# First attention by pairs of heads, and its output linear's first two tiles in parts

## The reference

```python
def diff_attention(h, w_qkv, w_o, lam_params, subln_g, rel_bias, lambda_init):
    qkv = h @ w_qkv
    ...
    logits = jnp.einsum('bqhmd,bkhmd->bhmqk', qb, k).astype(jnp.float32) * scale + bias
    logits = jnp.where(rel >= 0, logits, -jnp.inf)
    p = jax.nn.softmax(logits, axis=-1)
    w = p[:, :, 0] - lam * p[:, :, 1]
    return jnp.einsum('bhqk,bkhe->bqhe', w.astype(v.dtype), v)
    ...
    o = rms_norm(o, subln_g) * (1 - lambda_init)
    return o.reshape(b, s, A_V_WIDTH) @ w_o
```

## Time and profile before

| | |
|---|---|
| median of 3 runs | 2152.95 us (2150.6 to 2153.96) |
| profiled execution | 2148.51 us |
| its span, first to last instruction | 2146.7 us |
| PE busy | 1883.2 us (88%) |
| DVE busy | 1645.4 us (77%) |
| ACT busy | 876.8 us (41%) |
| POOL busy | 526.4 us (25%) |
| mean granted clock of PE | 0.938 |

### The profile page before, as it was taken

The page is one execution under the profiler, slowest core; times in us unless marked ns, Lnnn a source line. Parts: engine busy times, 40 slices in busy tenths (PEclk is TensorE's granted clock), DMA queues, the critical chain, the costliest instruction groups (busy, mean ns, idle before and its releaser), DMA issues.

```text
span 2146.7 us, 32722 instructions
## 1 busy us (share of the span) xinstructions
PE 1883.2 (88%) x12438; PEld 1589.1 (74%) x12438; DVE 1645.4 (77%) x2910; ACT 876.8 (41%) x1409; POOL 526.4 (25%) x464
## 2 busy tenths in 40 slices
PE   5999898999999998899999999999776766766676
PEld 5999897999999997899999999989422222222222
DVE  5887767887888877654569998758988877877765
ACT  3444465544555436654444445555212112212111
POOL 0111002111001110211120002332554455445451
PEclk7999999999999998999999999999988888888888
DMA  7889732678868884254544454536999999999996
GB/s 316 319 314 369 290 137 101 240 307 293 294 253 309 308 326 180 99 194 162 169 175 164 177 177 177 190 105 267 412 422 422 422 422 422 422 423 422 423 423 250
DMA packets 88787, 606.34 MB, mean 282 GB/s; under 512 B 9763, under 2 KB 11059, under 8 KB 21468
## 3 DMA queue, kind: packets, MB, share of 16 engines
q1 hardware_dynamic: 37708, 245.03, 31.8%
q0 software_dynamic: 37040, 270.57, 30.3%
q10 hardware_dynamic: 13920, 89.15, 10.3%
HBM read 601.53 MB, written 3.18 MB: 282 GB/s over the span
## 4 chain that ended last, share of the span: by engine, by line
PE 25%; DMA 22%; DVE 11%; issue 2%; ACT 2%; POOL 0%; DVEq 0%; POOLq 0%; ACTq 0%
DMA row_pair<-in_peer_uv,mod_ring 22%; PE ps L806 16%; PE ps L1270 3%; DVE w_lo L1877 3%; PE ps L837 2%; DVE work L2332 2%; DVE row_pair L2562 2%; DVE SQ L2332 2%; PE ps L869 1%; DVE work L1934 1%; PE ps L903 0%; ACT diag L1844 0%; PE ps L1007 0%; PE ps L1226 0%; ACT w_hi L1292 0%
## 5 line engine op out<-in xcount | busy, mean ns | idle before, releaser
L1877 DVE TENSOR_TENSOR w_lo<-raw,w_hi 128x2048 fp32r<-128x2048 f32 (+1 forms) x248 | 527.2, 2128 | 214.7 <-ACT w_hi L1292 214.2
L1270 PE MATMUL ps<-row_pair,diag 128*128 128x512 f32 x768 | 434.2, 726 | 189.8 <-ACT diag L1844 189.8
L1292 ACT ACTIVATE w_hi<-raw 128x2048 fp32r<-128x2048 f32 (+1 forms) x248 | 440.4, 1777 | 240.6 <-PE ps L806 175.2
L1270 PEld LDWEIGHTS ps<-row_pair,diag 128*128 128x128 f32 x768 | 173.2, 233 | 450.2 <-ACT diag L1844 240.7
L806 PE MATMUL ps<-HH,w_hi 128*128 128x256 f32 x1584 | 445.5, 281 | 0.0
L806 PE MATMUL ps<-HL,w_hi 128*128 128x256 f32 x1584 | 443.7, 280 | 0.0
L806 PE MATMUL ps<-HH,w_lo 128*128 128x256 f32 x1584 | 443.5, 280 | 0.0
L2562 DVE SCALAR_TENSOR_TENSOR row_pair<-row_pair,HTOK 128x1024 f32<-128x1024 f32 x256 | 313.7, 1226 | 131.7 <-DMA row_pair<-in_peer_uv,mod_ring 130.1
L778 POOL DMA_INDIRECT row_pair<-in_peer_uv,mod_ring x256 | 315.0, 1230 | 337.6 <-PE ps L1270 258.9
L806 PEld LDWEIGHTS ps<-HL,w_hi 128*128 128x128 f32 x1584 | 298.7, 189 | 0.0
L806 PEld LDWEIGHTS ps<-HH,w_hi 128*128 128x128 f32 x1584 | 297.4, 188 | 1.6 <-issue 1.3
(11 more groups left out here) (326 smaller groups left out, 3251.2 us busy)
## 6 DMA issues: line engine op xcount, KB each, us to landing
raw<-in_f_in SPq DMA_DIRECT2D x88, 1024.0 KB, 4.9
...
```

The source lines that it names most:

```text
L1270: last = mm(ps[:, 2 * t + c, :], diag[:, d, :], row_v(k)[:, c * 512:(c + 1) * 512], start=False, stop=False)
L1292: f(slot(w_hi, g), slot(raw, g), ACT.Copy).then_inc(hi_ready, 1)
L1877: v.tensor_tensor(slot(w_lo, g), slot(raw, g), f32(slot(w_hi, g)), ALU.subtract).then_inc(low["v"], 1)
```

## The change

All four pairs of heads get the same order: query tile, key tile and value tile of the pair, then the next pair's. The scores of the first head stand ahead of the value tile, those of the second between its halves; `a_turn` of the first head stands behind it, that of the second between the halves of the next query tile, with `a_values` of the first head; `a_values` of the second behind that tile; the pair's `squares_sum` between the halves of the next key tile. At the end the first two tiles of `a_o` are cut into parts over k (0 to 2, 3 to 5, 6 and 7), which stand between the last steps of heads 6 and 7, each k behind its wait for EL; `a_o` now uses four banks (6, 2, 1, 3) in turn. The squares of heads 6 and 7 are summed, rooted and normalized by head rather than by pair. ACT gets a `preload` of Exp behind each of three square roots.

```diff
-A_ORDER = [("q", 0), ("k", 0), ("q", 1), ("k", 1), ("v", 0), ("q", 2), ("k", 2), ("v", 1),
-           ("q", 3), ("k", 3), ("v", 2), ("v", 3)]
-A_BANKS = [(1, 3), (0, 2), (1, 3), (0, 1), (3, 0)] + [(1, 3)] * 7
+A_ORDER = [(kind, t) for t in range(4) for kind in "qkv"]
+A_BANKS = [(1, 3), (0, 2)] + [(1, 3)] * 10
...
-OWN_BANKS = {"x_q": (4, (2, 4))}
+OWN_BANKS = {"x_q": (4, (2, 4)), "a_o": (0, (6, 2, 1, 3))}
 OWN_BANKS.update({f"a_{kind}{t}": (0, banks) for (kind, t), banks in zip(A_ORDER, A_BANKS)})
...
-        SUB_BANK = (0, 0, 5, 7)
+        SUB_BANK = (0, 0, 0, 7, 4)
+        SUB_HEADS = (slice(0, 2), slice(2, 4), slice(4, 6), slice(6, 7), slice(7, 8))
...
-                if c in (2, 4):
+                if c in (2, 4, 6):
                     pe.wait_ge(sub_root, c // 2)
...
             def squares_sum(b):
 
                 pe.wait_ge(sub_sq, b + 1)
-                if b == 2:
-                    pe.wait_ge(logits_ready, 2 * STEP_END["A"])
-                mm(ps[:, SUB_BANK[b], :], ones[:, :], SQ[:, 2 * b:2 * b + 2, :], start=True, stop=True
+                heads = SUB_HEADS[b]
+                mm(ps[:, SUB_BANK[b], 0:SEQ * (heads.stop - heads.start)], ones[:, :], SQ[:, heads, :], start=True, stop=True
                    ).then_inc(sub_sum, 1)
 
+            def out_part(t, k0, k1):
+
+                ln = LIN["a_o"]
+                if k0 == 0:
+                    tile_wait(ln.tile0 + t)
+                    if t == 0:
+                        pe.wait_ge(logits_ready, 2 * STEP_END["A"])
+                w = wparts(ln.tile0 + t)
+                for m in range(2):
+                    q = ln.chunk0 + 2 * t + m
+                    if k0 == 0:
+                        freed_wait(q, None)
+                    for k in range(k0, k1):
+                        if m == 0:
+                            pe.wait_ge(el_ready, ESET["attA"] + k + 1)
+                        last = product(ps[:, BANK[q], 0:SEQ], lambda u, k: w[u][:, k, m * P:(m + 1) * P],
+                                       lambda u, k: (EH, EL)[u][:, k, :], k, k + 1, k == 0, k == DC - 1)
+                    if k1 == DC:
+                        last.then_inc(units_done, 1)
+
             def differential():
 
-                def query_or_key(name, between, behind, new=None):
-                    feat_tile(name, 0, mid=between, new=new)
-                    behind()
-
-                def value(name, between, behind):
-                    tok_tile(name, 0, mid=between)
-                    behind()
-
-                feat_tile("a_q0", 0, new="n1")
-                feat_tile("a_k0", 0)
-                query_or_key("a_q1", lambda: a_scores(0), lambda: a_scores(1))
-                query_or_key("a_k1", lambda: a_turn(0), lambda: a_turn(1))
-                value("a_v0", lambda: a_scores(2), lambda: a_scores(3))
-                query_or_key("a_q2", lambda: (a_values(0), a_turn(2)), lambda: a_values(1))
-                query_or_key("a_k2", lambda: a_turn(3), lambda: squares_sum(0))
-                value("a_v1", lambda: a_scores(4), lambda: a_scores(5))
-                query_or_key("a_q3", lambda: (a_values(2), a_turn(4)), lambda: a_values(3))
-                query_or_key("a_k3", lambda: a_turn(5), lambda: squares_sum(1))
-                value("a_v2", lambda: a_scores(6), lambda: a_scores(7))
-                value("a_v3", lambda: (a_values(4), a_turn(6)), lambda: a_values(5))
+                for p in range(4):
+                    a, b = 2 * p, 2 * p + 1
+                    if p == 0:
+                        feat_tile("a_q0", 0, new="n1")
+                        feat_tile("a_k0", 0)
+                    else:
+                        feat_tile(f"a_q{p}", 0, mid=lambda: (a_turn(a - 1), a_values(a - 2)))
+                        a_values(a - 1)
+                        feat_tile(f"a_k{p}", 0, mid=lambda: squares_sum(p - 1))
+                    a_scores(a)
+                    tok_tile(f"a_v{p}", 0, mid=lambda: a_scores(b))
+                    a_turn(a)
+                out_part(0, 0, 3)
                 a_turn(7)
                 a_values(6)
-                squares_sum(2)
+                out_part(1, 0, 3)
                 a_values(7)
                 squares_sum(3)
+                out_part(0, 3, 6)
+                squares_sum(4)
+                out_part(1, 3, 6)
+                out_part(0, 6, 8)
+                out_part(1, 6, 8)
...
-            pe.wait_ge(sub_root, 3)
-            residual("a_o", "attA", 2)
+            pe.wait_ge(sub_root, len(SUB_HEADS))
+            for t in range(2, 4):
+                feat_tile("a_o", t)
...
@@ (ACT, differential)
...
+                for p in range(4):
+                    a, b = 2 * p, 2 * p + 1
+                    split(g0 + 3 * p + 2)
+                    query(a)
+                    if p:
+                        a_copy(a - 1)
+                        a_output(a - 2)
+                    query(b)
+                    split(g0 + 3 * p + 3)
+                    if p:
+                        a_output(a - 1)
+                        sub_sqrt(p - 1)
+                        preload(ACT.Exp)
+                    if p > 1:
+                        sub_high(a - 4)
+                        sub_high(a - 3)
+                    split(g0 + 3 * p + 4)
+                    exps(a)
+                    value(p)
+                    exps(b)
+                    a_copy(a)
...
+                sub_high(4)
                 sub_sqrt(3)
+                sub_high(5)
+                sub_sqrt(4)
+                sub_high(6)
+                sub_high(7)
...
@@ (DVE, differential)
...
+                for p in range(4):
+                    a, b = 2 * p, 2 * p + 1
+                    split(g0 + 3 * p + 2)
+                    split(g0 + 3 * p + 3)
+                    key(a)
+                    key(b)
...
+                    logits(a)
+                    split(g0 + 3 * p + 4)
+                    logits(b)
+                    probs(a)
+                    if 0 < p < 3:
+                        sub_norm(a - 2)
+                    value(p)
+                    probs(b)
+                    if 0 < p < 3:
+                        sub_norm(a - 1)
```

113 lines of the change are left out of this document (9 added, 104 removed).

## The result

| | before | after |
|---|---|---|
| median | 2152.55 us of 4 runs (2150.60 to 2153.96) | 2138.12 us of 4 runs (2137.40 to 2138.50) |
| ratio, 95% interval | | 0.9935 (0.9919 to 0.9951) |
| profiled execution, span | 2148.51 us, 2146.7 | 2138.50 us, 2136.7 |

The change makes the kernel faster, by 14.4 us by medians, where the prediction said 10.6 and 2142.4 us. By these the gain is 11.0 or 10.5 us; the standard deviations of 2.7 and 2.9 us leave about 1.5 us on either side.

What follows compares the result with a forecast made beforehand. TensorE (PE) sets the pace; its 125.03 us stage holds 105.35 of work and 19.7 lost. Waits of 7.5 plus start-ups of 1.6 leave 9.1 lost, gaining 10.6: from 2152.95 to 2142.4 us, range 2138.5 to 2148.0.

Steps and rivals of the forecast that it cites:

- k = 4: In tile 0 of `a_o`, PE waits 1.4 us for EL of head 4, whose copy on ACT follows head 7's output.
- k = 5: In tile 0 of `a_o`, PE waits 0.5 us for another square root and copy, 0.84 against 0.36.
- k = 7: In `a_o`, PE waits 1.6 us: 4.1 us from the last sum of squares, against 2.5 of PE work.
- tile 2: Tile 2 of `a_o` waits 1.5 us, behind its own late split and the first residual, whose bank it reuses.
- next layer: The feed-forward layer's second chunk waits 0.7 us for the residual of `a_o`'s last chunk, whose bank it writes.
- start-ups: Matmuls starting up again after waits on PE: 0.2 us for each of eight waits, 1.6 us in all.
- a dense pair and three tiles: The stage's work on PE: four dense head pairs of 21.98 us plus three net tiles, 17.43, make 105.35 us.
- the tail rival: Last probabilities to last EL stay at 16.7 us, not 13.3, and the clock falls once: 2147.5 us; chance 0.07.
- The table rival: On ACT, switching tables costs twice its row, so turns of first heads wait 1.2, 2.0, 2.0: 2147.7 us; chance 0.03.
- the median of 2152.95, which lies 4.4 above it: Step from profiled execution to median: 2137.9 us predicted for the profiled execution becomes a median of 2142.4.
- The clock rival: PE's clock falls behind the new waits, three slow stretches at 1.7 us: 5.1 less gain, 2147.5 us; chance 0.10.
- The slower rival: Turns of heads 2 to 7 lose 3.45 + 1.7 us each behind their scores: 18.8 slower, 2171.8 us; chance 0.05.

Runs made afterwards that it cites:

- all edits: After with both norms behind the second head's probabilities in pairs 1 and 2, sums earlier in the end, eight `a_o` banks, and tile 2's split earlier; 2131.63 us.
- four loads: After with one more preload of the square-root table and one of the exponential table behind each pair's square root; 2146.34 us.

## Why the prediction was right, and where it was off

| step | predicted, us | profile of after, us |
|---|---|---|
| `a_turn(0)` | 0.3 | 0 |
| `a_turn(3)`, `a_turn(5)` | 0.75 each | 0.70, 0.69 |
| k = 4 | 1.4 | 1.25 |
| k = 5 | 0.5 | 0.07 |
| k = 7 | 1.6 | 1.59 |
| tile 2 | 1.5 | 1.22 |
| next layer | 0.7 | 1.48 |
| idle in all | 7.5 | 6.99 |
| start-ups | 1.6 | 1.81 |
| half clock | 0 | 0 |
| lost, and stage | 9.1, 114.4 | 8.80, 114.15 |

**What held.** The work of 105.35 us, read off as a dense pair and three tiles, is the basis of it all, and the kernel with all edits, whose stage takes 106.86 us with 1.1 of idle time in it, bears it out. The start-ups are what is left, 114.15 - 105.35 - 6.99 = 1.81; no row shows them by themselves. Six of the eight waits stand where the list has them, with its causes: the norms at the two turns (moved behind, the waits went; moved ahead, they grew by the 2.19 predicted for one), ACT's copy behind the output of head 7 at k = 4, the last root at k = 7, the late split at tile 2, the bank ahead of the next layer. From the end of DVE's last probabilities to that of the last EL (349.99 + 0.73 = 350.72, above) it took 13.3 us as worked out, against 16.7 in before, so the tail rival falls:

```profile
336.69 0.74 DVE L2107 SCALAR_TENSOR_TENSOR work<-work,rscale 128x128 f32<-128x128 f32 x2
```

The table rival falls by the rows of four loads, and in after the turns of heads 2, 4 and 6 wait for nothing.

**What was luck in the sum.** Two waits of the list, 0.3 us at `a_turn(0)` and 0.5 at k = 5, all but did not come, and those at k = 4 and tile 2 came out 0.15 and 0.28 shorter; the wait ahead of the next layer, 0.78 longer, made up for more than half of that. And the start-ups, priced at 0.2 us for each of eight waits, are 1.81 us for six, 0.3 each. That the stage came out within 0.3 us is in part such errors against each other.

**The term that was mis-sized** is the wait ahead of the next layer, 1.48 for 0.7. I priced one residual; on DVE the residuals of both last chunks stood behind HLX of chunks before them. I had not followed DVE's queue at that place. The trace of before has it: there, too, the last two residuals come back to back behind HLX,

```profile
375.50 0.86 DVE L2061 SCALAR_TENSOR_TENSOR X<-ps,mods,X 128x256 f32<-128x256 f32 x2
```

and end at 376.36, 1.24 us behind the next layer's first matmul at 375.12, which in six banks did not need them. With a hand-off that is about the 1.48. It cost nearly nothing in the end, for a reason that I had not seen either.

**What was overlooked.** I read 223.84 of 224.88 us as PE setting the pace behind the stage and let it be. The missing 1.04 us is one wait, for `w_lo` in the next layer's fourth tile. After does not have it: PE comes there later, by the wait ahead of the layer. Behind the stage the next layer takes 191.4 to 192.1 us in after's three profiles against 193.25 in each of before's two, 1.2 to 1.8 less. So the wait of 1.48 is in fact nearly free, and the prediction's step "what the stage loses on PE moves everything behind it one to one" holds only down to the next point that another engine sets.

**Why the time was still 4.3 us high.** The failing step is "the median of 2152.95, which lies 4.4 above it". I carried the distance between before's profiled execution and its median over to after, as if it belonged to the kernel. It belongs to the draw, of the execution or of the chip, which these runs do not tell apart: before lies anywhere from 2144.2 to 2157.3 us over 86 runs, after from 2135.2 to 2145.0 over 17, with the stage the same to 0.2 us in every profile of either. The three runs shown of before lay some 2 us high and the first four of after 2 us low. The lower end of the range had the same fault: it allowed 3 us for the waits and looked at a spread of 3.4 us in three runs. The draw of two medians, some 2 us each here, belonged into it. Over all runs the gain is 10.5 us by means, close to the 10.6 forecast; but the stage and the next layer together show 11.9 to 12.7, and whether the difference is more than the uncertainty of 1.5 stays open.

**The clock rival** did not come true in after, whose waits, none above 1.7 us, are followed by a clock of 1.00 in all three profiles. It was closer than the 0.10 that I gave it says: waits of 2.09 (twice), 2.14 and one of two of 2.89 us were followed by stretches of 0.50 in kernels that differ by one edit. **The slower rival** had the price of a turn too high: it put 1.7 us of half clock on each wait, and two waits made 2.2 us longer cost 5.8 us in that profile, 4.4 and the clock once. What felled it is that the long waits were not there.
